# The last block of a five-block transformer, rebuilt around its S5 scan

## What is computed

```python
xn = rms_norm_2(h, mix_norm)
q, k, v, gate_a, u, gate_s = split(xn @ w_in)        # six times 512 columns
attn = dilated_mixture_attention(q, k, v, q_norm, k_norm) * silu(gate_a)   # 8 heads of 64
ssm = s5_glu(u, ...) * silu(gate_s)
h = h + concat([attn, ssm]) @ w_out
gate = sigmoid(rms_norm_2(h, ple_norm) @ w_ple_gate)
h = h + gate * (p @ w_ple_proj)
# s5_glu: 32 groups of 16 channels, 64 complex states each; dt = exp(log_dt)
#   x[t] = a x[t-1] + B u[t] (complex, diagonal a), y = Re(C x) + d_skip * u
#   yg = gelu(y);  out = yg * sigmoid(yg @ w_glu + b_glu)
```

## Time and profile before

| | us |
|---|---|
| three runs | 1560.07, 1562.82, 1562.58 |
| median | 1562.58 |
| the profiled execution | 1560.26 |
| its span, first to last instruction | 1558.5 |

### The profile page before, as it was taken

One profiled execution on the slowest core, in us unless ns is written; L12 is line 12 of the kernel. 1 busy time (PEld: TensorE's weight loads), 2 busy tenths in 40 slices (PEclk: granted clock), 3 DMA queues, 4 the chain that ended last, 5 costly groups with the idle time before them and its releaser, 6 DMA issues.

```text
span 1558.5 us, 20465 instructions
## 1 busy us (share of the span) xinstructions
PE 1413.5 (91%) x6865; PEld 1152.5 (74%) x6865; DVE 1035.4 (66%) x1971; ACT 793.8 (51%) x1494; POOL 179.0 (11%) x313
## 2 busy tenths in 40 slices
PE   6898999999998999989899999998999999884288
PEld 5676888877887888778688887777888877662166
DVE  5987755567637555596565557987655569659845
ACT  5574644556636445566364455664654457530033
POOL 2000000000100000000000000000000009958600
PEclk9999999999999999999999999999999999956689
DMA  8533555545333655532265554542556545500021
GB/s 263 168 121 120 191 190 187 188 153 186 109 108 123 222 183 187 189 122 85 92 211 193 187 181 158 162 136 88 193 180 199 183 154 176 189 0 0 0 86 63
DMA packets 154226, 230.97 MB, mean 148 GB/s; under 512 B 7388, under 2 KB 102816, under 8 KB 154160
## 3 DMA queue, kind: packets, MB, share of 16 engines
q1 hardware_dynamic: 152176, 224.31, 43.9%
q0 software_dynamic: 1984, 5.82, 1.4%
HBM read 229.05 MB, written 1.05 MB: 148 GB/s over the span
## 4 chain that ended last, share of the span: by engine, by line
PE 77%; DVE 15%; ACT 3%; POOL 2%; issue 2%; DMA 0%; DVEq 0%; ACTq 0%; POOLq 0%
PE ps L1883 22%; PE ps L1885 22%; PE ps L1884 22%; DVE w_rest L1198 3%; PE ps L2482 1%; DVE x L1259 1%; PE ps L1903 1%; DVE pr L1415 1%; DVE qkv L1431 1%; ACT w_head L737 1%; ACT scr_a L725 1%; PE ps L2026 1%; DVE sc L1415 1%; PE ps L2382 1%; DVE qkv L1305 0%
## 5 line engine op out<-in xcount | busy, mean ns | idle before, releaser
L1883 PE MATMUL ps<-w_head,xt_head 128*128 128x512 f32 (+1 forms) x1368 | 540.2, 395 | 19.8 <-DVE xt_rest L1205 7.8
L1885 PE MATMUL ps<-w_head,xt_rest 128*128 128x512 f32 (+1 forms) x1368 | 528.1, 386 | 0.0
L1884 PE MATMUL ps<-w_rest,xt_head 128*128 128x512 f32 (+1 forms) x1368 | 527.1, 385 | 0.0
L1198 DVE SCALAR_TENSOR_TENSOR w_rest<-w_raw,gain_t,w_head 128x512 fp32r<-128x512 f32 (+1 forms) x600 | 400.5, 732 | 92.8 <-ACT w_head L737 92.2
L737 ACT ACTIVATE w_head<-w_raw,gain_t 128x512 fp32r<-128x512 f32 (+1 forms) x600 | 374.1, 700 | 152.8 <-PE ps L1885 143.0
L1883 PEld LDWEIGHTS ps<-w_head,xt_head 128*128 128x128 f32 x1368 | 259.1, 189 | 74.4 <-issue 10.9
L1885 PEld LDWEIGHTS ps<-w_head,xt_rest 128*128 128x128 f32 x1368 | 258.6, 189 | 52.9
L1884 PEld LDWEIGHTS ps<-w_rest,xt_head 128*128 128x128 f32 x1368 | 259.4, 190 | 47.5
L1196 DVE TENSOR_TENSOR w_rest<-w_raw,w_head 128x1024 fp32r<-128x1024 f32 x132 | 156.4, 1227 | 103.2 <-ACT w_head L737 103.2
L737 ACT ACTIVATE w_head<-w_raw 128x1024 fp32r<-128x1024 f32 x132 | 132.5, 1054 | 105.0 <-PE ps L1885 99.7
L1883 PE MATMUL ps<-w_head,ht_head 128*128 128x512 f32 x360 | 140.5, 390 | 5.6 <-DVE ht_rest L1720 5.6
(11 more groups left out here) (373 smaller groups left out, 1438.9 us busy)
## 6 DMA issues: line engine op xcount, KB each, us to landing
w_raw<-in_ffn_w_gate_dram SPq DMA_DIRECT2D x88, 512.0 KB, 4.0
w_raw<-in_ffn_w_up_dram SPq DMA_DIRECT2D x88, 512.0 KB, 4.9
w_raw<-in_ffn_w_down_dram SPq DMA_DIRECT2D x88, 512.0 KB, 4.2
w_raw<-in_a_w_in_dram SPq DMA_DIRECT2D x48, 512.0 KB, 4.7
w_raw<-in_b_w_in_dram SPq DMA_DIRECT2D x24, 512.0 KB, 4.7
w_raw<-in_w_in_dram SPq DMA_DIRECT2D x24, 512.0 KB, 4.7
w_raw<-in_a_w_out_dram SPq DMA_DIRECT2D x16, 512.0 KB, 4.2
w_raw<-in_c_w_in_dram SPq DMA_DIRECT2D x10, 512.0 KB, 4.5
```

The costliest lines, as they stand in the source:

```text
L1198: ins = dve.scalar_tensor_tensor(w_rest[:, s, w], w_raw[:, s, w], by, hd, ALU.mult, ALU.subtract)
L1883: pe.matmul(out_, hd, wh, start=first, stop=False)
L1884: pe.matmul(out_, hd, wr, start=False, stop=False)
L1885: return pe.matmul(out_, rt, wh, start=False, stop=last)
```

## The change

- **Order of the projection** (`L_ORDER`): u first, then q, k, v, gate_a, gate_s. `dilated` replaces `linear`, `attend`, `exps`, `softmaxes`, `s5_scan` and `glu` on PE, ACT and VectorE. All chunks use PSUM banks 0 and 1, a bank per half of the tokens (`half_unit`), so that PE's second half covers the first one's copy.
- **S5** in eight half groups: `turned_in` (six operations of 512 elements) and `turned_out` (four scans, four operations), all on VectorE, between weight rests and attention; PE's `driven` and `readout` stand between units. GpSimd does nothing in the block.
- **Tables**: `powers` at the end of layer 2's FFN, `tables` for all groups in the FFN of layer 4, where p is loaded too. B and C are loaded and widened in the FFN of layer 2 (`b_widened`, `c_widened`) and turned ahead of the entries of layers 3 and 4 (`s5_weights_turned`).
- **Attention**: the key counts enter as logarithms in the mask, in two parts (`masks_r`, `share_rest`), so that VectorE's products with the counts go and PE adds two mask products per pair. Squares of q and k come from 32 small ACT operations with accumulators. One pair at a time, in banks 2, 3 and 7.
- **fp32 parts**: p's projection, the attention half of the output product and the GLU are made as plain fp32 products straight from `w_raw` (`project`, `out_a`, `glu`), without head and rest. The GLU is transposed (channels on partitions), its sigmoid a tanh; the S5 half of the output (`out_s`) keeps the three products.
- **p's projection** moves from the tail into the block and is copied out (`proj`).
- **Elsewhere**: `gain` has one buffer, loaded behind each use; four more transfers for b_glu and the q and k gains and one more row stand among the gain rows at the start, and PE waits for 11.

The diff, cut to its core (leading spaces cut too):

```diff
...
+L_ORDER = (4, 0, 1, 2, 3, 5)
+L_UNITS = 12
+PROJ, OUT_A, GLU, OUT_S = L_UNITS, L_UNITS + 1, L_UNITS + 3, L_UNITS + 4
+RAW_UNITS = 4
...
-pool.wait_ge(sq_done, SQUARES)
-for g_ in range(3):
-    tables(g_)
...
+        if i + 1 < ADDS:
+            post_gain(i + 1)
+        if i == 2:
+            s5_loads()
+        elif i == 3:
+            powers()
+        elif i == 6:
+            pool.dma_start(p_tok, a["p_2"][0, 0].rearrange("(m p) c -> p m c", p=P)).then_inc(p_in, 16)
+            for g_ in range(4):
+                tables(g_)
...
+    head(u + 3)
+    act.wait_ge(rstd_done, n["rstd"])
+    out_of(0, tok[:, :, 512:1024], ACT.Copy)
+    head(u + 4)
+    turned(u_t[:, 0:2, :], 6)
+    turned(u_t[:, 2:4, :], 7)
+    head(u + 5)
+    out_of(1, tok[:, :, 0:512], ACT.Copy)
+    head(u + 6)
+    squares(0)
+    turned(p_turned, 6)
+    head(u + 7)
+    out_of(2, tok[:, :, 512:1024], ACT.Copy)
+    head(u + 8)
+    squares(1)
+    head(u + 9)
+    act.wait_ge(qk_sq, 2)
+    out_of(3, v_d, ACT.Copy)
+    head(u + 10)
+    turned(q_t[:, 0:2, :], 2)
+    turned(k_t[:, 0:2, :], 3, qk_gain)
+    head(u + 11)
+    out_of(4, ga_d, ACT.Silu)
+    turned(q_t[:, 2:4, :], 7)
+    exp(0)
+    turned(k_t[:, 2:4, :], 7, qk_gain)
+    spread_out(0)
+    out_of(5, gs_d, ACT.Silu)
+    exp(1)
+    proj_copied(0)
+    turned(gs_t[:, 0:2, :], 7)
+    spread_out(1)
+    exp(2)
+    proj_copied(1)
+    turned(gs_t[:, 2:4, :], 7)
+    spread_out(2)
+    o_copied(0)
+    exp(3)
+    act.preload_act_table_set("gelu_and_others")
+    gelu(0)
+    gelu(1)
+    spread_out(3)
+    gelu(2)
+    o_copied(1)
+    head(u + OUT_S)
+    head(u + OUT_S + 1)
+    gelu(3)
+    gate(0)
+    gate(1)
+    ssm_copied(0)
+    gate(2)
+    ssm_copied(1)
+    gate(3)
+    ssm_copied(2)
+    ssm_copied(3)
+    u += OUT_S + 2
+    n["x"] += 4
+    n["bank"] += 2
+    head(u - 3 + RING)
+    head(u - 2 + RING)
...
+    def turned_in(h):
+        g, half = h // 2, h % 2
+        cs, sn = half_tiles(g, half)
+        t_, z0, z1, _ = s5_piece[h]
+        br, bi = ps[:, 4:6, 0:TOK], ps[:, 4:6, TOK:2 * TOK]
+        dve.wait_ge(tab_done, 4)
+        dve.wait_ge(bu_ready, h + 1)
+        if h >= 2:
+            dve.wait_ge(y_ready, h - 1)
+        dve.tensor_tensor(t_, bi, sn, ALU.mult)
+        step(dve.tensor_tensor(z0, br, cs, ALU.mult))
+        dve.tensor_tensor(z1, bi, cs, ALU.mult)
+        step(dve.tensor_tensor(z0, z0, t_, ALU.add))
+        dve.tensor_tensor(t_, br, sn, ALU.mult).then_inc(bu_taken, 1)
+        dve.wait_ge(bu_taken, h + 1)
+        step(dve.tensor_tensor(z1, z1, t_, ALU.subtract))
+    def turned_out(h):
+        g, half = h // 2, h % 2
+        cs, sn = half_tiles(g, half)
+        t_, z0, z1, e_ = s5_piece[h]
+        for z in (z0, z1):
+            for i in range(2):
+                decay = s5[:, DECAY, 2 * h + i:2 * h + i + 1].to_broadcast([P, TOK])
                 last = dve.tensor_tensor_scan(z[:, i, :], decay, z[:, i, :], 0.0, ALU.mult, ALU.add)
-            last.then_inc(done, 1)
-        scan(z_st[0], z0_scanned)
-        if g == BUSY:
+        step(last)
+        dve.tensor_tensor(t_, z0, cs, ALU.mult)
+        if h:
+            dve.wait_ge(y_ready, h)
+        step(dve.scalar_tensor_tensor(e_, z1, -1.0, sn, ALU.mult, ALU.mult))
+        dve.tensor_tensor(z0, z0, sn, ALU.mult)
+        dve.tensor_tensor(z1, z1, cs, ALU.mult).then_inc(xs_done, 1)
...
+    rest(u + 3)
+    rest(u + 4)
+    turned_in(0)
+    rest(u + 5)
+    turned_out(0)
+    rest(u + 6)
+    turned_in(1)
+    rest(u + 7)
+    turned_out(1)
+    rest(u + 8)
+    qk_norm()
+    turned_in(2)
+    rest(u + 9)
+    y_out(0)
+    turned_out(2)
+    rest(u + 10)
+    peak(0)
+    turned_in(3)
+    rest(u + 11)
+    peak(1)
+    turned_out(3)
+    gated(0)
+    y_out(1)
+    turned_in(4)
+    turned_out(4)
+    peak(2)
+    gated(1)
+    turned_in(5)
+    turned_out(5)
+    peak(3)
+    gated(2)
+    y_out(2)
+    turned_in(6)
+    turned_out(6)
+    gated(3)
+    ssm_part(0)
+    turned_in(7)
+    turned_out(7)
+    ssm_part(1)
+    y_out(3)
+    ssm_part(2)
+    rest(u + OUT_S)
+    step(ssm_part(3))
+    ssm(0)
+    ssm(1)
+    ssm_rest_of(0)
+    ssm(2)
+    ssm_rest_of(1)
+    ssm(3)
+    ssm_rest_of(2)
+    ssm_rest_of(3)
+    rest(u + OUT_S + 1)
...
+    pe.wait_ge(gain_rows_in, 16 * 11)
...
+    def half_unit(s, m):
+        j, half = s // 2, s % 2
+        if not half:
+            pe.wait_ge(in_out, 2 * j - 1 + m)
+        for t in range(4):
+            pe.wait_ge(rest_done, 4 * (u + s) + t + 1)
+            last = product(ps[:, m, :], XT, 4 * half + t, m, (u + s) % RING, 512 * t, 512, half + t == 0, half == 1 and t == 3)
+        if m:
+            last.then_inc(unit_used, 1)
+        elif half:
+            last.then_inc(in_half, 1)
...
-    pe.wait_ge(gain_rows_in, 16 * 6)
...
+    def driven(h):
+        if h:
+            pe.wait_ge(bu_taken, h)
+        g, half = h // 2, h % 2
+        for c in range(2):
+            for i in (2 * half, 2 * half + 1):
+                r_ = slice(32 * i, 32 * i + 32)
+                last = pe.matmul(ps[:, 4 + i % 2, TOK * c:TOK * c + TOK], b_t[r_, c, g, :], u_t[r_, g, :], start=True, stop=True)
+        last.then_inc(bu_ready, 1)
+    def readout(h):
+        pe.wait_ge(xs_done, h + 1)
+        k, half = h // 2, h % 2
+        if k:
+            pe.wait_ge(y_done, k)
+        re_cos, re_sin, im_cos, im_sin = s5_piece[h]
+        for j, (c, z) in enumerate(((0, re_cos), (0, im_sin), (1, re_sin), (1, im_cos))):
+            for i in range(2):
+                r_ = slice(64 * half + 32 * i, 64 * half + 32 * i + 32)
+                last = pe.matmul(ps[r_, 6, 0:TOK], c_t[:, c, k, r_], z[:, i, :], start=j == 0, stop=j == 3, skip_group_check=True)
+        last.then_inc(y_ready, 1)
     def scores(t):
-        b = t % 2
-        if t >= 2:
-            pe.wait_ge(e_done, n["pair"] + t - 1)
+        half = [slice(HD * c, HD * c + HD) for c in range(2)]
         for c in range(2):
-            r = slice(HD * c, HD * c + HD)
-            kb = k_t[r, t, :]
-            pe.matmul(ps[:, 2 * b + c, 0:MAP], ident_r[:, :], mask, start=True, stop=False, skip_group_check=True)
-            pe.matmul(ps[:, 2 * b + c, 0:TOK], q_t[r, t, P:2 * P], kb, start=False, stop=True, skip_group_check=True)
-            last = pe.matmul(ps[:, 2 * b + c, TOK:MAP], q_t[r, t, 0:P], kb[:, 0:P], start=False, stop=True, skip_group_check=True)
+            pe.matmul(ps[:, 2 + c, 0:MAP], ident_r[:, :], masks_r[:, i_:i_ + MAP], start=True, stop=False, skip_group_check=True)
+            pe.matmul(ps[:, 2 + c, 0:MAP], ident_r[:, :], share_rest[:, :], start=False, stop=False, skip_group_check=True)
+        for c, r_ in enumerate(half):
+            pe.matmul(ps[:, 2 + c, 0:TOK], q_t[r_, t, P:2 * P], k_t[r_, t, :], start=False, stop=True, skip_group_check=True)
+        for c, r_ in enumerate(half):
+            last = pe.matmul(ps[:, 2 + c, TOK:MAP], q_t[r_, t, 0:P], k_t[r_, t, 0:P], start=False, stop=True, skip_group_check=True)
         last.then_inc(s_ready, 1)
...
+    def project(m):
+        raw_there(u + PROJ)
+        for j in range(2):
+            for t in range(2):
+                last = pe.matmul(ps[:, j, :], p_turned[:, t, P * m:P * m + P], raw_w(u + PROJ, 1024 * t + 512 * j, 512), start=t == 0, stop=t == 1)
+            if (m, j) != (1, 1):
+                last.then_inc(proj_ready, 1)
+        return last
+    def out_a(c, tiles, m):
+        unit = u + OUT_A + c
+        raw_there(unit)
+        for t in tiles:
+            last = pe.matmul(ps[:, out_unit(c, m), :], o_t[:, t, P * m:P * m + P], raw_w(unit, 512 * t, 512), start=t == 0, stop=False)
+        return last
+    def glu(k):
+        raw_there(u + GLU)
+        pe.wait_ge(yg_done, k + 1)
+        for j in range(4):
+            last = pe.matmul(glu_bank(j), raw_w(u + GLU, 512 * k + P * j, P), yg[:, k, :], start=k == 0 and j < 3, stop=k == 3,
+                             skip_group_check=True)
+            if k == 3 and j < 2:
+                last.then_inc(glu_ready, 1)
+        return last
...
+    half_unit(2, 0)
+    pe.wait_ge(in_out, 2)
+    turn_group(tok[:, :, 512:1024], 0, 6)
+    turn_group(tok[:, :, 512:1024], 1, 7)
+    half_unit(2, 1)
+    half_unit(3, 0)
+    pe.wait_ge(turn_used, tr + 2)
+    driven(0)
+    half_unit(3, 1)
+    half_unit(4, 0)
+    pe.wait_ge(p_in, 16)
+    turn_group(p_tok, 0, 6)
+    half_unit(4, 1)
+    driven(1)
+    half_unit(5, 0)
+    half_unit(5, 1)
+    pe.wait_ge(turn_used, tr + 3)
+    readout(0)
+    half_unit(6, 0)
+    half_unit(6, 1)
+    driven(2)
+    half_unit(7, 0)
+    half_unit(7, 1)
+    readout(1)
+    half_unit(8, 0)
+    pe.wait_ge(qk_normed, 1)
+    turn_group(tok[:, :, 0:512], 0, 2)
+    pe.wait_ge(qk_normed, 2)
+    turn_group(tok[:, :, 512:1024], 0, 3)
+    half_unit(8, 1)
+    driven(3)
+    half_unit(9, 0)
+    pe.wait_ge(turn_used, tr + 5)
     scores(0)
-    pe.wait_ge(evac_a, n["ev_a"])
-    for t in range(N + 2):
```

(98 more changed lines are left out.)

798 lines of the change are left out of this document (322 added, 476 removed).

## The result

The changed kernel takes **1476.03 us** (median of 4 runs, 1472.1 to 1482.46), the kernel before 1562.7 us on the same chip (4 runs, 1560.07 to 1564.02). The ratio is 0.9445, with a 95% interval of 0.9423 to 0.9466. The forecast was 1493, its range 1474 to 1526. So the direction and the range hold, and the size is 17 us off. The profiled execution took 1474.92 us, its span is 1472.3 us, 86.2 less than before.

What follows compares the result with a forecast made beforehand. TensorE was taken to bound the kernel up to 1358 and VectorE from 1393 to 1487, a latency chain between; 1298.5 + 150 + 10.9 + 29.7 = 1489.1 us of span, so 1493.2 us, range 1474 to 1526.

Steps and rivals of the forecast that it cites:

- stretch 2: Merged middle, last block's unit 2 to first product of output's S5 half: 138 us plus 12 for clock, 150 us.
- stretch 1: Everything before unit 2 of the last block: +6.1 us, so that unit 2 begins at 1298.5.
- stretch 3: The products of the output's S5 half: 48 products, 10.9 us.
- Rival A: The clock stays full, without the 12 us for a lower clock: 1481 us; chance 0.24 with its floor.
- (a): Kernel start: first weight head waits for all gain rows, five transfers added on POOL's queue: +2.5 us, bounds 0 and +4.
- (b): Ahead of layers 3 and 4 PE turns eight blocks and waits for two ACT copies: +2.6 us, bounds 0 and +5.
- (c) and (d): VectorE's widening of B in layer 2's FFN and GpSimd's rotation tables in the last: together +1 us, bounds 0 and +10.
- B: The clock stays low from unit 11 to the output's S5 half: 1526 us; chance 0.12.
- D: As a rival: slower than before, holes between pieces keep the clock low from unit 2 on: 1580 us; chance 0.04.
- C, lockstep: In each half group VectorE waits for PE's drive and readout, nothing hidden: 1509 us; chance 0.15.

Runs made afterwards that it cites:

- Serial: Changed kernel with S5 half groups 0 to 3 put behind all projection rests and units, same instructions, only the interleaving undone: 1500.87 us, ratio 0.9591 to before.
- pairs first: Changed kernel with the four attention pairs run without S5 half groups between them, half groups 4 to 7 after: 1502.53 us, ratio 0.9628 to before.
- Thin: Changed kernel with half of the middle's fp32 products (p's projection, output's attention half, GLU) left out: 1479.13 us, ratio 0.9464 to before.
- no tables: Changed kernel with the rotation tables filled by constants in place of GpSimd's doubling steps in layer 4's FFN: 1477.14 us, ratio 0.9469 to before.
- readout early: Changed kernel with readout(7) ahead of GLU's first three quarters and the last gelu between the output's two weight heads: 1481.24 us, ratio 0.9485 to before.
- peak late: Changed kernel with one line moved in VectorE's queue, the second peak after turned_out(3): 1477.84 us, ratio 0.9453 to before.
- GpSimd load: Changed kernel with 80 unused GpSimd products of 512 elements added from the first drive on: 1531.6 us, ratio 0.9811 to before.
- after again: The changed kernel itself, unedited, timed a second time: 1478.51 us over 6 runs, ratio 0.9460 to before.

## Why the prediction came out as it did

**The mechanism** was as forecast: TensorE bound up to the scores of the second pair, VectorE 90% busy from 1309 to 1420 with hardly a hole otherwise, half groups of 9.1 us (forecast 8.9), scans 0.6 us apart, and nothing of GpSimd in the block. The end of half group 7 was put at 1416 on the old clock; it came at 1416.5. VectorE's hole before the second peak was put at 6 us (4.72), readout(7) at 1421 (1423.1, with unit 2 about one us later), the tail at 29.7 (29.7). Serial and pairs first show that the overlap carries much of the gain: with part of it undone 19.9 and 27.8 us come back, which would be 48 of the 76 us of stretch 2 if they add up (8.4 of them from the place of one drive, and with what the lower clock costs in both); no run undoes both at once. The other 28 were not tried. By the rows some 10 of them are cheaper half groups (eight of 9.1 us in place of the four groups' 82.6); the rest would be work that left the path (the output's attention half, GLU, the key counts), which is argued and not shown.

**Stretch 2, the clock: the step that failed.** The forecast of 1493 was 17 us too long: by the spans 5 in stretch 1 and 13 in stretch 2, less 2 in stretch 3. The sum of stretch 2 took 138 us at full clock and added 12 for a clock of 0.75 after unit 11. It came as 136.6, and the clock was 1.00 in every window from 1293 to 1430. Other profiles of the same order have one short fall there, worth 1.5 us: the term was 0 to 1.5 and not 12. The argument for the 12 was "only pieces of 1 to 3.4 us with holes". Thin shows that even with half of the long pieces gone the clock keeps to 1.00 from 1350 to 1430 but for those 4 us near 1382; serial shows 0.51 where TensorE is busy 14.87 of 28 us with holes of 3 to 5 us, and pairs first 0.57 where it is busy 12.93 of 24. In the kernel after it is busy 28.5 of 31 and 32.3 of 37 us, and its longest hole after unit 11 is 2.02 us. The prediction had both numbers, 50.6 us of work in 57 to 60 us of time, and should have read them as a nearly gapless queue. Rival A (1481) was the right case and had 0.24; that the time came out 5 us below even A is stretch 1. The range held, but the forecast's own case, a clock of 0.7 to 0.8, did not occur. The Trainium skill (TensorE: Matmul & The Clock Gate, Why this matters for your kernels) warns of idle gaps between bursts, and serial and pairs first agree with it (holes of 3.5 to 4.7 and of 3.8 to 4.3 us). The one short fall of the other profiles stands behind a hole of only 2.02 us, and not in every execution. I had counted as such gaps what the kernel doesn't have.

**Stretch 1: +6.1 forecast, +1.3 measured.** (a) The start: the first product moved from 14.30 to 16.03, +1.7 for 2.5. (b) The turned weights: +2.6 forecast. Between the fourth turns of entries the stretch with layer 3's turns grew by 0.16 us (190.47 to 190.63) and that with layer 4's by 0.33. The kernel after, entry of layer 3:

```profile
670.59 1.11 PE L1974 MATMUL ps<-const,x 128*128 128x128 f32 x8 [0.88 <-ACT b_t L1076]
...
675.83 0.66 PE L1974 MATMUL ps<-const,x 128*128 128x128 f32 x4 [1.48 <-DVE x L1333]
```

The wait for ScalarE's copies is there (0.88), but TensorE then waits for VectorE's third sum all the same, 1.48 us now and 1.74 before. I had priced the delay of the first turn and not asked what is late next. (c) and (d) +1 forecast, 0 measured (no tables). Not in the sum at all: unit 2 waits 0.84 us for ScalarE's copy of u, whose banks it takes over. That makes +3.1. The remaining -1.8 is luck with the clock of the two profiled executions: before has stretches at 0.5 near 52, 771, 1053 and 1087, after has three, all before 125 us. By the distances between the same turns the two more at the start cost the kernel after 2.4 us, and it is spared 2.6 near 771 and 1.5 near 1053; the one near 1087 costs nothing, as it ends before a wait for VectorE.

**Stretch 3**: 10.9 forecast, 12.7 measured: one low-clock stretch (0.87 over 1430 to 1443) after the hole of 1.84 us. The profiles without it have 11.0.

**The rivals.** B and D fell, the clock stayed. C, lockstep, fell too: VectorE has one hole of 1.02 us at a `y_out` and none at a half group between 1304 and 1417 but for the peak's. A lower bound from TensorE's work was missing from the argument. Its own prices give 119 us of it in stretch 2 (54.5, 14 and 50.6), and the trace has 129.4: readout early and peak late show that its holes, not VectorE's larger ones, set what is left.

**The price of GpSimd beside VectorE** was given from the earlier trace rows as one scan in four at 2.8 us and the others at 0.66. That misreads the rows: half of the scans of `sc` took over 0.89 us. It also leaves out the larger loss. Kernel before, the first group, with GpSimd helping (two rows of VectorE and GpSimd's own), then group 1, where VectorE does all operations itself:

```profile
1408.00 4.50 DVE L1415 TENSOR_TENSOR_SCAN pr<-s,pr 128x256 f32<-128x256 f32 x4
...
1412.59 3.24 POOL L704 TENSOR_TENSOR q_t<-pr,q_t 128x1024 f32<-128x1024 f32 x1 [1.79 <-DVE pr L1415]
1413.55 3.36 DVE L1431 SCALAR_TENSOR_TENSOR qkv<-pr,scr_a 128x1024 f32<-128x1024 f32 x1
...
1430.35 1.33 DVE L1431 SCALAR_TENSOR_TENSOR qkv<-pr,gain 128x1024 f32<-128x1024 f32 x1
```

Four scans take 4.5 us in place of 2.4 to 2.6, and the operation of L1431 takes 3.36 in place of 1.33 while GpSimd's runs. The three groups that GpSimd helps take 19.3, 26.6 and 19.4 us, the one that it doesn't help, where it works on the fourth table meanwhile, 17.3: the help cost VectorE more than the operations that it took over. The load of GpSimd load shows the same at 1.35 to 1.52 us for operations of 0.69, for as long as GpSimd runs.

## What to carry to other kernels

Where two engines' queues are merged, add up each one's work and its holes: here the engine with few and short holes was the bound and kept its clock, and a large hole on the other engine is worth no more than the bound engine's own idle time beside it. When a helper engine slows the one that sets the path, its work belongs into a stretch where that one has time to spare: the same tables cost nothing in an FFN, and a like load 47 us beside a chain on VectorE. An early semaphore that collects many small transfers should be split by first use.

## What the hardware showed that was not expected

**The scatter of the runs goes largely with TensorE's clock.** Stretches of 3 to 8 us at 0.5 appear in one execution and not in the next of the same program, one or two in the first 60 us and none (pairs first) to seven (peak late) between there and the last block, and cost up to 2.7 us each. Over the six runs of after again the mean clock goes from 0.998 (1473.17 us) to 0.987 (1480.75 and 1484.17 us), about 1 us for each 0.001. It is not the whole: readout early took 1475.22 us at 0.985 and 1484.77 at 0.984. What sets off a stretch stays open. A comparison of two kernels by one run each is blind below 10 us here; D, a distance between two events inside the trace, repeats to 0.03 us.
